# Layer norm and first choice of experts by token tile, in a two-block transformer kernel on one core

## The reference

```python
x = layer_norm(DEEPNORM_ALPHA * x + gate * f, ln_g[i, 0], ln_b[i, 0])
shift, scale, gate = ada_mod(c, ada_w[i, 1], ada_b[i, 1])
h = x * scale + shift
f = peer_ffn(h, peer_w_q[i], peer_sub_keys[i], peer_u[i], peer_v[i])
...
q = (xc @ w_q).reshape(PEER_CHUNK, PEER_HEADS, 2, PEER_HALF)
s = jnp.einsum('thpd,pnd->thpn', q, sub_keys).astype(jnp.float32)
sv, si = lax.top_k(s, PEER_TOPK)
cand_s = (sv[:, :, 0, :, None] + sv[:, :, 1, None, :]).reshape(...)
top_s, pos = lax.top_k(cand_s, PEER_TOPK)
idx = jnp.take_along_axis(cand_i, pos, axis=-1)
g = jax.nn.softmax(top_s, axis=-1).astype(xc.dtype)
act = jax.nn.gelu(jnp.einsum('td,thkd->thk', xc, u[idx]), approximate=False)
return jnp.einsum('thk,thkd->td', g * act, v[idx])
```

## Time and profile before

| | us |
|---|---|
| median of 3 runs | 2375.33 |
| lowest and highest | 2371.5, 2378.37 |
| span of the profiled execution | 2643.4 |
| TensorE busy in it | 2537.3 |
| VectorE busy | 1595.0 |
| ScalarE busy | 1111.4 |
| GpSimd busy | 702.4 |
| mean granted clock of TensorE | 0.741 |

### The profile page before, as it was taken

The page is one execution under the profiler, slowest core; times in us unless marked ns, Lnnn a source line. Parts: engine busy times, 40 slices in busy tenths (PEclk is TensorE's granted clock), DMA queues, the critical chain, the costliest instruction groups (busy, mean ns, idle before and its releaser), DMA issues.

```text
span 2643.4 us, 28258 instructions
## 1 busy us (share of the span) xinstructions
PE 2537.3 (96%) x9756; PEld 1535.3 (58%) x9756; DVE 1595.0 (60%) x3700; ACT 1111.4 (42%) x2732; POOL 702.4 (27%) x624
## 2 busy tenths in 40 slices
PE   7879999999999999999999999999999999999998
PEld 7758999777999998644333334443334443333432
DVE  4554566656556676856667537536726554677665
ACT  4353433425443333444444436434426443445443
POOL 0000001010001100744555224324423333444443
PEclk7667777777777777777777777777777777777777
DMA  5203467452447754899999999999989997999997
GB/s 208 80 1 126 154 218 284 166 183 88 135 168 252 258 198 134 314 362 396 420 420 420 346 342 378 347 339 413 410 317 344 357 349 289 421 420 420 421 420 309
DMA packets 131348, 768.22 MB, mean 291 GB/s; under 512 B 14480, under 2 KB 16272, under 8 KB 59280
## 3 DMA queue, kind: packets, MB, share of 16 engines
q0 software_dynamic: 87552, 587.24, 56.3%
q1 hardware_dynamic: 42944, 177.81, 19.6%
q10 hardware_dynamic: 720, 1.51, 0.2%
HBM read 765.45 MB, written 1.05 MB: 290 GB/s over the span
## 4 chain that ended last, share of the span: by engine, by line
PE 84%; DMA 7%; ACT 4%; DVE 3%; issue 1%; SPq 0%; ACTq 0%; POOL 0%; DVEq 0%
PE bank L904 34%; PE bank L547 11%; PE bank L548 10%; PE bank L549 10%; PE bank L938 8%; DMA arena<-experts,arena 7%; PE bank L679 1%; PE bank L659 1%; PE bank L626 1%; PE bank L647 1%; ACT L1421 1%; DVE arena L2268 1%; PE bank L576 1%; ACT L1431 1%; ACT arena L1240 0%
## 5 line engine op out<-in xcount | busy, mean ns | idle before, releaser
L904 PE MATMUL bank<-arena 128*128 128x512 f32 x2048 | 1204.8, 751 | 26.4 <-ACT arena L1426 24.3
L2268 DVE CUSTOM_DVE_ANT_0 arena<-arena 128x1024 f32<-128x1024 f32 x512 | 636.5, 1245 | 542.3 <-DMA arena<-experts,arena 541.5
L513 POOL DMA_INDIRECT arena<-experts,arena x512 | 617.9, 1207 | 908.7 <-PE bank L904 873.9
L904 PEld LDWEIGHTS bank<-arena 128*128 128x128 f32 x2048 | 411.1, 206 | 759.5 <-issue 599.3
L1166 ACT CAST whi<-wring 128x1024 fp32r<-128x1024 f32 x228 | 238.1, 1048 | 372.4 <-PE bank L549 361.5
L1685 DVE TENSOR_TENSOR wlo<-wring,whi 128x1024 fp32r<-128x1024 f32 x216 | 263.3, 1224 | 207.4 <-ACT whi L1166 207.1
L1421 ACT ACTIVATE arena<-arena 128x1 f32<-128x1 f32 x512 | 102.6, 200 | 441.5 <-DVE arena L2268 439.4
L499 POOL DMA_DIRECT2D arena<-ada_w x64 | 34.0, 532 | 789.5 <-DVE adaM L1732 771.2
L1426 ACT ACTIVATE arena<-tab,arena 128x128 f32<-128x128 f32 x512 | 205.5, 401 | 16.7
L547 PE MATMUL bank<-hTh,whi 128*128 128x256 f32 (+1 forms) x576 | 190.9, 331 | 16.8 <-DVE hTl L1694 9.3
L938 PE MATMUL bank<-wring,hfT 128*128 128x512 f32 x320 | 188.6, 746 | 0.0
(11 more groups left out here) (327 smaller groups left out, 3264.6 us busy)
## 6 DMA issues: line engine op xcount, KB each, us to landing
wring<-w_stream SPq DMA_DIRECT2D x236, 512.0 KB, 3.5
wring<-w_stream SPq DMA_DIRECT2D x48, 1024.0 KB, 6.8
arena<-ada_w POOLq DMA_DIRECT2D x64, 512.0 KB, 4.8
alibi<-ada_w POOLq DMA_DIRECT2D x32, 512.0 KB, 4.7
arena<-experts,arena POOLq DMA_INDIRECT x512, 10.6
xT<-xT_in SPq DMA_DIRECT2D x1, 1088.0 KB, 5.2
alibi<-alibi_in ACTq DMA_DIRECT2D x1, 1024.0 KB, 5.4
tab<-tab_in SPq DMA_DIRECT2D x1, 831.0 KB, 6.6
```

The costliest lines, as they stand in the source:

```text
L513: pool.indirect_dma_start(g_ring[:, r], None, experts[n // (2 * PEER_HEADS)], bass.IndirectOffsetOnAxis(idx[:, s // SLOTS % 2, s % SLOTS:s ...
L904: last = mm(banks[2 * t + b][:, :], diag[:, r], g_ring[:, r, D + b * TILE_N:D + (b + 1) * TILE_N], start=s % SLOTS == 0, stop=s % SLOTS == ...
L2268: v.tensor_tensor_reduce(g_ring[:, r, 0:D], g_ring[:, r, 0:D], hrow[:, t], 1.0, 0.0, ALU.mult, ALU.add, act8[:, r:r + 1]).then_inc(dot_don ...
```

## The change

The sums of the layer norm are made for each tile of 128 tokens by itself, and tile 0 is taken through the norm, two query chunks, the scores of head 0 and `select_head(0)` ahead of tile 1. Chunks 0 and 1 are therefore computed in two halves of 128 tokens. Tile 1's modulation moves behind `select_head(0)` on DVE. `x2` is written by ACT (`Identity` with scale and bias) instead of DVE. On POOL no low part stands ahead of the first gather: eight gathers come first, with `hrow_done` ahead of the seventh and `ln_done` ahead of the eighth, because the arrays of the norm now lie in ring places 6 and 7. On ACT the high parts of the next weight group stand behind both copies of a pair of chunks. DVE does four dot products ahead of `select_head(1)` and four inside it. `BESIDE_HEAD` becomes 4, 4, 4, 6, 8, 10, 10, 6, again 52. The loads of group `G_PQ+2` wait for four chunks (`CHUNK_FREE`). The waits whose counts shift with it (`SC_FIRST`, `XS_FIRST`, `scores_no`) are the rest.

```diff
-BESIDE_HEAD = (0, 0, 0, 10, 14, 14, 14, 0)
-LOW_BESIDE = {12: 0, 14: 1, 22: 2, 24: 3}
+BESIDE_HEAD = (4, 4, 4, 6, 8, 10, 10, 6)
+LOW_AFTER = {7: ((1, 0), (1, 1)), 8: ((1, 2),), 9: ((1, 3),), 12: ((2, 0),), 14: ((2, 1),), 16: ((2, 2),), 18: ((2, 3),),
+             22: ((3, 0),), 24: ((3, 1),), 26: ((3, 2),), 28: ((3, 3),)}
+TICKS_AT_ONCE, FIRST_TICKS = 4, 8
...
+        CHUNK_FREE[G_PQ] = (4, 4, 3, 4)
+        SC_FIRST, XS_FIRST = PEER_HEADS + 1, 2
+        def scores_no(t, h):
+            return (1, 3)[t] if h == 0 else 2 if h == 1 else h + 2
...
-            for c in range(CPT):
-                split_lo(G_PQ + 1, c)
-            pool.wait_ge(ln_done, 8)
             for s in range(N_SLOTS):
-                if s == 3:
+                if s == 6:
                     pool.wait_ge(hrow_done, 4)
+                elif s == 7:
+                    pool.wait_ge(ln_done, 8)
                 gather(s)
-                if s in (1, 2, 4, 6):
-                    split_lo(G_PQ + 2, s // 2)
-                elif s in LOW_BESIDE:
-                    split_lo(G_PQ + 3, LOW_BESIDE[s])
...
-                    last = mm(banks[4][:, 0:SEQ], table("ones_mean"), xnT[:, kc], start=kc == 0, stop=kc == KC - 1)
-                last.then_inc(mean_done, 1)
-                for kc in range(KC):
-                    pe.wait_ge(sq2_done, 8 * i + kc + 1)
-                    last = mm(banks[5][:, 0:SEQ], table("ones_mean"), sq2T[:, kc], start=kc == 0, stop=kc == KC - 1)
-                last.then_inc(var_done, 1)
+                    ready(kc)
+                    last = mm(banks[bank][:, 0:P], table("ones_mean"), src[:, kc, t * P:(t + 1) * P], start=kc == 0,
+                              stop=kc == KC - 1)
+                last.then_inc(done, 1)
+            def first_layer_norm():
+                for t in range(2):
+                    tile_sums(4 + 2 * t, xnT, t, after(xn_ready, 0), mean_done)
+                for t in range(2):
+                    tile_sums(5 + 2 * t, sq2T, t, lambda kc: pe.wait_ge(sq2_done, 2 * t + kc // 4 + 1), var_done)
...
+            first_layer_norm()
...
             def query_chunk(c):
                 if c >= 4:
-                    pe.wait_ge(pq_copied, c - 3)
-                chunk(G_PQ + c // CPT, c % CPT, banks[(2, 3, 6, 7)[c % 4]][:, 0:SEQ], pq_in, after(mod_split, 8) if c == 0 else None)
-            def head_scores(y):
-                if y == 0:
+                    pe.wait_ge(pq_copied, c + 1 if c < 6 else c - 1)
+                query_products(c, 0, SEQ, after(mod_split, 16) if c == 2 else None, 0 if c == 3 else 1)
+            def turned_input(t):
+                pe.wait_ge(hf_ready, t + 1)
+                for c in range(KC):
+                    if t and c % 4 == 0:
+                        pe.wait_ge(hrow_copied, c // 4 + 1)
+                    last = nc.tensor.transpose(banks[c // 4][:, (c % 4) * P:(c % 4 + 1) * P], hf[:, c, t * P:(t + 1) * P], ident)
+                    if c % 4 == 3:
+                        last.then_inc(hrow_done, 1)
...
-            for h in range(PEER_HEADS + 1):
-                if h < PEER_HEADS:
+            query_products(0, 0, P, after(mod_split, 8), 1)
+            query_products(1, 0, P, None, 1)
+            head_scores(0, (0,))
+            turned_input(0)
+            query_chunk(2)
+            query_chunk(3)
+            turned_input(1)
+            pe.wait_ge(pq_copied, 1)
+            query_products(0, P, SEQ, None, 0)
+            head_scores(1)
+            pe.wait_ge(pq_copied, 2)
+            query_products(1, P, SEQ, None, 1)
+            pe.wait_ge(hrow_copied, 4)
+            for h in range(1, PEER_HEADS + 1):
+                if h == 2:
+                    head_scores(0, (1,))
+                elif h >= 3:
+                    head_scores(h - 1)
+                if 2 <= h < PEER_HEADS:
                     query_chunk(2 * h)
-                if h >= 2:
-                    head_scores(h - 1)
-                if h < PEER_HEADS:
                     query_chunk(2 * h + 1)
-                if h == 0:
-                    head_scores(0)
...
-                if h == 3:
-                    pe.wait_ge(hrow_copied, 4)
...
+            def first_layer_norm():
+                af(warm[:, :], vcol("eps", 0), ACT.Sqrt)
+                for t in range(2):
+                    for half in range(2):
+                        act.wait_ge(xc_done, 2 * t + half + 1)
+                        piece = (slice(None), slice(4 * half, 4 * half + 4), slice(t * P, (t + 1) * P))
+                        af(sq2T[piece], xnT[piece], ACT.Square).then_inc(sq2_done, 1)
+                tile_root(0)
...
+                tile = slice(t * P, (t + 1) * P)
...
+                    act.wait_ge(mod_ready, 8 + 8 * t + kc + 1)
+                    af(hTh[:, kc, tile], hf[:, kc, tile], ACT.Identity, bias=both_b[:, 0, kc:kc + 1]).then_inc(mod_hi, 1)
...
@@ -1592,66 +1635,81 @@
                 split_hi(G_CONV + 5 + kc // CPT, kc % CPT)
             split_his(G_COUT + 1)
             split_his(G_COUT + 2)
-            layer_norm(0)
             act.dma_start(skT, subkeys[0]).then_inc(sk_landed, 16)
-            act.wait_ge(mod_ready, 9)
+            first_layer_norm()
+            modulated_hi(0)
...
-                    query_hi(c)
+            def query_copy(c, n0=0, n1=SEQ):
+                if c == 3:
+                    act.wait_ge(hrow_done, 4)
+                else:
+                    act.wait_ge(lin_done, CPT * G_PQ + (4 if n0 else c + 1))
+                nc.scalar.copy(pqT[:, c // 2 % 2, c % 2, n0:n1], banks[(2, 3, 6, 7)[c % 4]][:, n0:n1]).then_inc(pq_copied, 1)
             def query_hi(c):
-                split_hi(G_PQ + c // CPT + 1, c % CPT)
...
-                if s % PK == 2 and s < (TURNS - 1) * PK:
...
-            for h in range(PEER_HEADS + 1):
-                if h < PEER_HEADS:
-                    if h >= 2:
-                        act.wait_ge(sk_done, h - 1)
+            query_copy(0, 0, P)
+            query_copy(1, 0, P)
+            copy_scores(0, 0, 1)
+            copy_input(0)
+            modulated_hi(1)
+            gate_exp(0)
+            query_copy(2)
+            copy_input(1)
+            query_copy(3)
+            copy_scores(1)
+            act.wait_ge(xs_done, 2)
+            for c in range(KC):
+                af(x2[:, c], xnT[:, c], ACT.Identity, scale=vcol("ln_g", c), bias=vcol("ln_b", c)).then_inc(ln_done, 1)
+            for h in range(1, PEER_HEADS + 1):
+                if h == 2:
+                    query_hi(0)
+                    query_hi(1)
+                    query_copy(0, P, SEQ)
+                    query_copy(1, P, SEQ)
+                    query_hi(2)
+                    query_hi(3)
+                    copy_scores(0, 1, 2)
+                elif h >= 3:
+                    copy_scores(h - 1)
+                if 2 <= h < PEER_HEADS:
+                    act.wait_ge(sk_done, scores_no(1, h - 2))
                     query_copy(2 * h)
-                if h >= 2:
-                    copy_scores(h - 1)
-                if h < PEER_HEADS:
                     query_copy(2 * h + 1)
-                if h == 0:
-                    copy_scores(0)
-                if 2 * h + 1 < 12:
-                    query_hi(2 * h + 1)
-                if 1 <= h < 3:
-                    t = h - 1
-                    for b in range(2):
-                        act.wait_ge(hrow_done, 2 * t + b + 1)
-                        nc.scalar.copy(hrow[:, t, b * TILE_N:(b + 1) * TILE_N], banks[b][:, :]).then_inc(hrow_copied, 1)
-                if h == 3:
-                    gate_exp(0)
+                    if 2 * h < 12:
+                        query_hi(2 * h)
+                        query_hi(2 * h + 1)
                 for _ in range(BESIDE_HEAD[h - 1] if h else 0):
                     coefficient(early)
...
+            def modulated(t):
+                tile = slice(t * P, (t + 1) * P)
                 for n in range(KC + 2):
...
+            def first_input(t):
+                tile = slice(t * P, (t + 1) * P)
+                dve.wait_ge(mod_split, 16 + 8 * t)
+                v.tensor_tensor(hf[:, :, tile], hf[:, :, tile], both_b[:, 0].unsqueeze(2).to_broadcast([P, KC, P]),
+                                ALU.add).then_inc(hf_ready, 1)
+            def tile_inverse(t):
+                tile = slice(t * P, (t + 1) * P)
+                dve.wait_ge(rt2_done, t + 1)
+                link(v.reciprocal(rinv[:, 0, tile], rt[:, 0, tile]))
+            def first_layer_norm():
+                dve.wait_ge(xn_ready, 8)
+                for t in range(2):
+                    dve.wait_ge(mean_done, t + 1)
+                    for half in range(2):
+                        piece = (slice(None), slice(4 * half, 4 * half + 4), slice(t * P, (t + 1) * P))
+                        v.tensor_tensor(xnT[piece], xnT[piece], banks[4 + 2 * t][:, 0:P].unsqueeze(1).to_broadcast([P, 4, P]),
+                                        ALU.subtract).then_inc(xc_done, 1)
```

(23 more changed lines are left out.)

125 lines of the change are left out of this document (56 added, 69 removed).

## The result

Before: 2375.8 us. Changed: 2394.7 us, from 2389.8 to 2396.6 in four runs. The ratio is 1.0080, with a 95% interval of 1.0063 to 1.0097: 19 us slower. The forecast was 2378, no change that can be told.

The account below looks back on a forecast made before the run. TensorE bounds it to 1033 us, gathers from 1250, both nearly between. At the upper clock DMA engines bind: 25.5 us idle against 23, 2.5 slower than 2375.3, so 2378; range 2364 to 2394.

Parts of the forecast that it names:

- The clock of the timed runs: Whole kernel: timed runs have nearly the upper clock level, while the profile's granted clock was 0.74.
- The first gather: After the layer norm and select_head(0): moves 14.7 us ahead at the profile's clock, some 13 at the upper clock.
- TensorE's side: Up to the 52nd slot, at the profile's clock: it ends 8.5 + 10.7 = 19 us later.
- the hole and the halves: TensorE's query chunks 0 to 3: idle before chunk 2 and chunks 0 and 1 in halves lose 8.5 us.
- At the upper clock: the DMA engines bind: From 1040 on: TensorE's 167 us become 125 against 130 of gathers plus about 20 of weight tiles; 2.5 us slower.
- 15 + 5.5 + 5 = 25.5: DMA idle time, new order: 15 before gathers, 5.5 in new stops, 5 for two slow restarts; 23 before.
- The 20.8 us of waits for ACT: TensorE's eight entries into slots: copies, high parts, coefficients and x2 cost 20.8 us together, 10.7 more than before.
- What the earlier gather is worth: DMA engines from 1040 to the first gather: idle time 15 us instead of 23.
- Rival (b): TensorE's order decides through the hole, halves and waits behind high parts: costs 7 to 19 us, 2390; chance 0.30.
- the hole of 9.3: TensorE before chunk 2: stands still 9.3 us for tile 1's low parts, which DVE starts after select_head(0).
- when slots wait over 3 us after each pair: One of two conditions under which TensorE's order decides; the other is a timed clock below about 0.9.
- the 268 us: Difference of profiled span 2643.4 and median 2375.3, read as the timed runs' higher clock; counted against TensorE's order deciding.

Follow-up runs that it names:

- e10_before_nolow: Kernel before with POOL's twelve low parts cut to 8 of 1,024 columns and TensorE reading the high part in their place: 2366.0 us, ratio 0.9975.
- e0_before: Kernel before, unchanged, profiled once more; that execution spans 2370.5 us at a mean granted clock of 0.967; timed 2372.3 us.
- e1_high: Changed kernel with ACT's first high part of a pair between the two copies, the second behind the second coefficient: 2377.9 us, ratio 1.0022.
- e3_tile1: Changed kernel with tile 1's modulation on DVE and its high parts on ACT ahead of select_head(0): 2389.1 us, ratio 1.0070.
- e4_both: Changed kernel with the edits of e1_high and e3_tile1 together: 2376.4 us, ratio 1.0014.
- e8_order: e4_both with second halves of chunks 0 and 1 ahead of chunk 2, weight ring freed earlier, some high and low parts moved: 2376.5 us, ratio 1.0023.
- e11_half: Changed kernel with each pair's first high part still behind both copies, the second moved behind the second coefficient: 2390.1 us, ratio 1.0075.
- e6_beside: e4_both with slots 8, 0, 0, 12, 12, 10, 10, 0, which also put the first four high parts behind eight coefficients: 2393.1 us, ratio 1.0082.
- e12_before_high: Kernel before with the high parts beside chunks 8 and 10 moved from between the two copies to behind both: 2375.1 us, ratio 1.0015.

## Why the prediction was wrong, step by step

**The clock of the timed runs** was read rightly: 0.96 to 0.97.

**The first gather.** `select_head(0)` took 8.7 us (910.76 to 919.46), forecast 8.8. The timelines of DVE, before and after:

```profile
914.40 0.47 DVE L2086 MAX8 arena<-arena 128x8 f32<-128x128 f32 x2
...
917.15 2.24 DVE L2108 TENSOR_TENSOR arena<-arena 128x256 f32<-128x256 f32 x1
919.42 2.27 DVE L2112 CAST arena<-arena 128x32 f32<-128x32 uint32 x1
...
926.87 0.17 DVE L2132 CAST arena<-arena 128x16 uint32<-128x16 f32 x1
```

```profile
910.76 0.49 DVE L2162 MAX8 arena<-arena 128x8 f32<-128x128 f32 x2 [5.17 <-ACT arena L1661]
...
919.29 0.17 DVE L2208 CAST arena<-arena 128x16 uint32<-128x16 f32 x1
```

The first gather came 11.1 us earlier, forecast 13. The stalls were POOL's: in e10_before_nolow, without its low parts, the same two operations take 0.41 and 0.18. The Trainium skill (SBUF — State Buffer, SBUF: two separate sides) says that DVE and GpSimd share a pair of ports which one instruction holds alone; these rows agree, an operation of 0.4 us lasting as long as a low part of 2.4.

**TensorE's side** was right in its single terms: a hole of 8.72 (forecast 9.3), waits of 3.2 to 4.6 ahead of five entries (3.3 ahead of four and 3.4 ahead of the first forecast), a half chunk about as long as a whole one (929.30 to 932.01, 2.7 us at 2.4 GHz; 2.8 for 256 columns). Its sum, +19, is also what was measured, and that is in part luck. The forecast had 10.7 us more of waits for ACT, 8.5 for the hole and the halves, and nothing for the clock. Up to gather 60 TensorE's waits for ACT grew by 2.6 us (26.7 to 29.3) and those for DVE by 4.4 (5.4 to 9.8), and its busy time by 10.2, of which the 48 matmuls more that the halves make, at 0.11 us, are 5. Most of the rest is the lower clock.

**The step that failed** is "At the upper clock: the DMA engines bind", with its sum 15 + 5.5 + 5 = 25.5 us of idle time against 23. It is 2.5 us more; measured were 14.8 more, 43.4 against 28.6. I let TensorE's 167 us shrink to 125, set 150 us of transfers against them, and took TensorE to have slack. The 20.8 us of waits for ACT from the same text were left out: with them it is 146 against 150. Measured from the end of the halves (935.74) to gather 60, TensorE took 174 us, 145 busy and 29 waiting, so that it was later than the transfers. Two things were wrong. First, the waits for ACT are ACT's microseconds and don't shrink with the clock. Those of 0.9 us and more ahead of slots, up to gather 60, are 10.1 us in the prediction's count for the kernel before, and 21.9 in e0_before; in the changed kernel 28.0 against 20.8. Second, the trace of before showed a granted clock of 0.65 to 0.75 in all stretches, busy or not, so it could not show that the timed runs have a clock that falls to 0.50 about a wait and stays there for microseconds of work. Idle time that is new behind the first gather was 17.1 us (20.7 against 3.6) instead of 10.5. e1_high, which moves only two high parts on ACT at each of four entries, returns 12.7 of it and 14 of the 19 us: 7.6 us of waiting and 7.7 of lower clock.

**What the earlier gather is worth** was the second error, of like size: I put it at 8 us less idle time (23 to 15), and it was 2.3 us (25.0 to 22.7). The old order moved 4.7 MB ahead of its first gather, 3.3 of them weight tiles, and the new one 2.0 MB, 0.6 of them weight tiles. The prediction named the weight tiles that now move among the gathers, and gave them no term in the sum. (It also takes 23 where it worked out 22, and 15 where 1058 - 1040 - 5 is 13; the difference of 8 is hardly touched by that.) The two errors together, 5.7 and 6.6 us, are the 12.3 us between 2.5 and 14.8.

**Rival (b)** came nearest: TensorE's order decides, and 19 us is the upper end of the 7 to 19 that I gave it. Of its parts the waits behind high parts counted; the hole of 9.3 hardly did (e3_tile1 2 us, and e4_both is not to be told from e1_high), and the clock was not among them. Its condition, "when slots wait over 3 us after each pair", was worked out in the same text for four of eight entries and measured at five, and I weighed it by the 268 us instead.

**What stays open.** With the long waits behind high parts gone, the hole gone and the DMA engines idle 3 us less than before (e8_order), the changed order still is 1.0023 of before. Deferred transfers explain some 3 us at gather 60; that the interval excludes 1.000 isn't explained by one row. And the length of a wait alone doesn't tell whether the clock falls: 2.27 us kept it in e0_before at 981.64 and lost it in e11_half at 959.69; 2.30 lost it in e0_before at 969.19 and 2.01 in e3_tile1 at 915.85; 2.74 us kept it in e1_high. What decides isn't shown. Nor is it whether fewer, longer batches of slots would pay (e6_beside).

## What to carry to other kernels

Where two engines hand over in turn, whatever the slower hand-over engine does just ahead of the first item (a cast, a table, a copy) costs its time and often TensorE's clock as well: put it behind the second item (14 of 19 us here). An earlier first transfer is worth only the idle time that it removes (2.3 us for a lead of 11.1), so compare the bytes moved before it in both orders. When an experiment changes how many items a batch has, look at what else hangs on the batch. And check, before choosing between two limits, whether the trace has the clock of the timed runs: waits for another engine don't scale with it.

## What the runs showed of the hardware

TensorE's granted clock fell to 0.50 at many waits of 2.0 to 4.6 us. It fell in the wait (at 938.9 in the changed kernel, in a wait from 935.74 to 940.10) or up to 0.7 us behind its end (at 983.0 in e12_before_high, where the wait ends at 982.35). 3.4 to 5.5 us of 128x512 matmuls then ran at 1.2 GHz: sixteen took 8.8 to 9.9 us instead of 7.1. The Trainium skill (TensorE: Matmul & The Clock Gate, Part 1) says that this clock follows how busy the engine has been; the trace agrees in that the drops come with waits, and waits of like length with and without a drop show that the last wait alone doesn't decide. An execution at a steady granted clock of about 0.74, as the first profile of before was, hides this entirely. GpSimd's subtraction of 128x1024 elements (2.4 us) beside two VectorE operations made these last 2.24 and 2.27 us instead of 0.41 and 0.18. A ring of eight places that fills up during three pairs of chunks without a slot cost the DMA engines 1.9 us (e6_beside).
